# The memory's normalisation and the first cross attention's keys projected at the program's start

## What is computed

```python
# first layer's start: modulation from c, a product with a 1024 x 9216 matrix per layer
mod = silu_c @ w_ada[layer] + b_ada[layer]
h = modulate(rmsnorm(x, norm_g[layer, 0]), sh1, sc1)
x = x + 0.5 * g1 * swiglu(h, ffn_w1[layer, 0], ffn_w3[layer, 0], ffn_w2[layer, 0])
...
# each of the four layers of the second kind, after its mixer
x = x + memory_cross_attention(rmsnorm_2(x, ln_xattn[i]), rmsnorm_2(mem, ln_mem[i]),
                               xa_q[i], xa_kv[i], xa_o[i]).astype(x.dtype)
```

## Time and profile before

| | |
|---|---|
| Time, median of 3 runs | 3674.41 us (3674.11 to 3675.62) |
| The profiled execution, its time | 3674.21 us |
| its span | 3672.5 us |
| PE busy | 3623.0 us, 99% |
| DVE busy | 1836.2 us, 50% |
| ACT busy | 747.8 us, 20% |
| mean granted clock of PE | 0.995 |
| bytes moved | 599 MB, 163 GB/s over the span |

### The profile page before, as it was taken

One profiled execution on the slowest core, in us unless ns is written; L12 is line 12 of the kernel. 1 busy time (PEld: TensorE's weight loads), 2 busy tenths in 40 slices (PEclk: granted clock), 3 DMA queues, 4 the chain that ended last, 5 costly groups with the idle time before them and its releaser, 6 DMA issues.

```text
span 3672.5 us, 46373 instructions
## 1 busy us (share of the span) xinstructions
PE 3623.0 (99%) x20180; PEld 2754.1 (75%) x20180; DVE 1836.2 (50%) x3184; ACT 747.8 (20%) x1468; POOL 15.6 (0%) x43
## 2 busy tenths in 40 slices
PE   7999999999999999999999999999999999999999
PEld 6946696894679587588866679677667977757795
DVE  7854387683536445125732227547412663532384
ACT  1004300101520053211121211033311113421110
POOL 1000000000000000000000000000000000000000
PEclk9999999999999999999999999999999999999999
DMA  9663478654234433334442334433233443333342
GB/s 389 252 261 127 155 280 315 256 184 169 107 128 161 183 115 115 138 138 154 168 160 92 142 135 161 171 127 115 93 135 119 161 181 141 115 129 146 136 169 103
DMA packets 42490, 598.99 MB, mean 163 GB/s; under 512 B 4736, under 2 KB 4752, under 8 KB 6192
## 3 DMA queue, kind: packets, MB, share of 16 engines
q1 hardware_dynamic: 41024, 589.94, 43.2%
q0 software_dynamic: 1264, 6.10, 0.4%
HBM read 594.97 MB, written 1.05 MB: 162 GB/s over the span
## 4 chain that ended last, share of the span: by engine, by line
PE 97%; DVE 1%; DMA 1%; ACT 0%; issue 0%; SPq 0%; DVEq 0%
PE ps L1366 12%; PE ps L2795 12%; PE ps L616 11%; PE ps L499 9%; PE ps L392 8%; PE ps L478 5%; PE ps L2253 4%; PE ps L519 3%; PE ps L2286 3%; PE ps L812 3%; PE ps L2695 3%; PE ps L1761 2%; PE ps L1781 2%; PE ps L3022 2%; PE ps L1756 2%; PE ps L829 2%
## 5 line engine op out<-in xcount | busy, mean ns | idle before, releaser
L616 PE MATMUL ps<-hT,ring 128*128 128x128 f32 (+1 forms) x3136 | 407.9, 292 | 0.0
L616 PEld LDWEIGHTS ps<-hT,ring 128*128 128x128 f32 x3136 | 392.7, 192 | 18.3 <-issue 3.8
L499 PE MATMUL ps<-ring,aT 128*128 128x512 f32 x784 | 341.5, 593 | 0.0
L499 PEld LDWEIGHTS ps<-ring,aT 128*128 128x128 f32 x784 | 148.0, 190 | 178.4 <-issue 178.2
L478 PE MATMUL ps<-ring,aT 128*128 128x512 f32 x448 | 197.4, 598 | 0.0
L228 DVE SCALAR_TENSOR_TENSOR memT<-big,silu_c,memT 128x512 f32<-128x512 f32 x238 | 178.8, 751 | 8.0
L541 ACT ACTIVATE big<-x 128x1024 f32<-128x1024 f32 x34 | 35.9, 1057 | 698.6 <-DVE x L593 389.9
L2253 PE MATMUL ps<-hT,ring 128*128 128x256 f32 x768 | 171.6, 380 | 0.0
L2253 PEld LDWEIGHTS ps<-hT,ring 128*128 128x128 f32 x768 | 144.9, 190 | 25.6 <-issue 7.6
L478 PEld LDWEIGHTS ps<-ring,aT 128*128 128x128 f32 x448 | 84.8, 192 | 100.8 <-issue 100.8
L2795 PE MATMUL ps<-big 128*128 128x128 f32 x1152 | 140.4, 275 | 0.0
(11 more groups left out here) (575 smaller groups left out, 5701.0 us busy)
## 6 DMA issues: line engine op xcount, KB each, us to landing
ring<-weights_in SPq DMA_DIRECT2D x244, 2048.0 KB, 7.8
big<-ada_in SPq DMA_DIRECT2D x34, 2048.0 KB, 8.1
ring<-ada_in SPq DMA_DIRECT2D x2, 2048.0 KB, 26.4
big<-b_gate_in POOLq DMA_DIRECT2D x1, 1536.0 KB, 17.5
x<-x_in SPq DMA_DIRECT2D x1, 1024.0 KB, 4.9
big<-b_gate_in POOLq DMA_DIRECT2D x1, 1024.0 KB, 8.7
big<-mem_in POOLq DMA_DIRECT2D x1, 1024.0 KB, 5.3
out<-big SPq DMA_DIRECT2D x2, 512.0 KB, 2.6
```

The lines of the kernel that those rows point to most:

```text
L499: last = pe.matmul(ps[:, 2 * t + half, :], aT[:, 4 * c + k, t * P:(t + 1) * P], w[:, k, half * 512:(half + 1) * 512], start=first, stop=(4 ...
L616: last = pe.matmul(ps[:, bank + m // 2, (m % 2) * SEQ + at:(m % 2) * SEQ + at + n], w[:, k, m * P:(m + 1) * P], hT[:, k, at:at + n], start ...
```

## The change

The memory is the first load of all and goes to `aT`. ACT and DVE normalise it ahead of x, PE transposes it first, and ACT and DVE take it out of PSUM twice: multiplied by the first cross attention's gain (`early_gained`) and plain (`early_mem`). PE projects the keys of cross attention 0 with two chunks that now lead the list of weights, so that all later chunks have numbers higher by 2 until cross attention 0. The transposes of x stand between the two key chunks; the reductions of slices 0 and 2 stand before the last quarter of the second.

GpSimd's queue writes memory and keys to device memory (`spill`, 2 MB in three parts) and only then issues the small loads, which wait for slice 3 in place of slice 2. memT is read back where the memory was loaded before, and the keys after the last tile of the first mamba is turned. All slices have two places in `big`, so slice 1 waits for the sum of slice 0, and slice 3 for that of slice 2. The ring holds chunks only. In `up_right_dve` of the first swiglu DVE waits for the spill. The fourth swiglu has no work on the memory. `down_pe` 6 ends without keys, and `xattn_pe` 0 projects the queries per token half with `first_channels_pe`.

```diff
+            mem_pe(pe)
+            pe.wait_ge(mem_act_done, 4)
+            pe.wait_ge(mem_dve_done, 4)
+            for j in range(2):
+                w = arrived(pe, j).rearrange("p (k c) -> p k c", k=KT)
+                for m in range(4):
+                    if (j, m) == (1, 3):
+                        pe.wait_ge(down_k_done, 1)
+                        for a in (0, 2):
+                            ada_reduce_pe(pe, a, ada_bank(4 + a // 2))
+                    for k in range(KT):
+                        last = pe.matmul(ps[:, 4 + 2 * j + m // 2, (m % 2) * SEQ:(m % 2 + 1) * SEQ], w[:, k, m * P:(m + 1) * P], early_gained(k), start=(k == 0), stop=(k == KT - 1))
+                last.then_inc(chunks_used, 1)
+                for t in range(TT if j == 0 else 0):
+                    pe.wait_ge(norm_dve_done, 3 * t + 3)
...
-            pool.wait_ge(ada_loaded[2], 16)
+            pool.wait_ge(mem_act_done, 4)
+            pool.wait_ge(mem_dve_done, 4)
+            pool.dma_start(spill[:, 0:2048], early_mem.rearrange("p k c -> p (k c)")).then_inc(mem_moved, 16)
+            for j in range(2):
+                pool.wait_ge(down_k_done, j + 1)
+                pool.dma_start(spill[:, 2048 + 1024 * j:3072 + 1024 * j], early_keys(j).rearrange("p m c -> p (m c)")).then_inc(mem_moved, 16)
+            pool.wait_ge(ada_loaded[1], 32)
...
-            if a >= 4:
-                sp.wait_ge(ada_step, 8 * ada_turn(a - 4) + 8 if a < 6 else 8 * (a - 1))
+            turn = ada_turn(a)
+            if turn >= 2:
+                sp.wait_ge(ada_step, 8 * (turn - 1))
...
             up_ready(dve, i)
+            if i is None:
+                dve.wait_ge(chunks_used, 2)
+                dve.wait_ge(mem_moved, 48)
...
         def keys_pool(pool):
+            pool.wait_ge(mix_turned, 4)
+            pool.dma_start(view(big, 2048, 2048), spill[:, 2048:4096]).then_inc(keys_loaded, 16)
...
         def xattn_pe(pe, n, i, c0):
-            for j in range(2):
+            if n == 0:
+                first_channels_pe(pe, i, c0)
+                pe.wait_ge(keys_loaded, 16)
+            for j in range(2 if n else 0):
...
+            sp.dma_start(view(aTf, 0, TT, D), mem_in.rearrange("(t p) d -> p t d", p=P)).then_inc(mem_loaded, 16)
+            sp.dma_start(col[:, :], col_in).then_inc(columns_loaded, 16)
+            chunk_load(sp, 0)
             sp.dma_start(x[:, :, :], x_in.rearrange("(t p) d -> p t d", p=P)).then_inc(x_loaded, 16)
-            sp.dma_start(col[:, :], col_in).then_inc(columns_loaded, 16)
-            for a in (0, 2):
-                ada_load(sp, a)
-            for c in range(2):
-                chunk_load(sp, c)
-            for a in (1, 3):
-                ada_load(sp, a)
+            ada_load(sp, 0)
+            chunk_load(sp, 1)
+            ada_load(sp, 2)
+            chunk_load(sp, 2)
+            ada_load(sp, 1)
+            chunk_load(sp, 3)
+            ada_load(sp, 3)
```

More of the change, by code:

```diff
@@ L672, in mem_take_act @@
                 for k in range(4 * g + 2, 4 * g + 4):
-                    last = act.copy(memT[:, k, :], ps[:, 2 * g + 1, (k % 2) * SEQ:(k % 2 + 1) * SEQ])
+                    turned = ps[:, 5 + 2 * g, (k % 2) * SEQ:(k % 2 + 1) * SEQ]
+                    act.activation(early_gained(k), turned, ACT.Identity, scale=column('ln_mem_2', k))
+                    last = act.copy(early_mem[:, k, :], turned)
                 last.then_inc(mem_act_done, 1)
@@ L691, in mem_take_dve @@
                 for k in range(4 * g, 4 * g + 2):
-                    last = dve.tensor_copy(memT[:, k, :], ps[:, 2 * g, (k % 2) * SEQ:(k % 2 + 1) * SEQ])
+                    turned = ps[:, 4 + 2 * g, (k % 2) * SEQ:(k % 2 + 1) * SEQ]
+                    dve.tensor_scalar(early_gained(k), turned, column('ln_mem_2', k), None, ALU.mult)
+                    last = dve.tensor_copy(early_mem[:, k, :], turned)
                 last.then_inc(mem_dve_done, 1)
@@ L1417, in first_halves_pe @@
             for j in range(2):
+                if j and not half:
+                    pe.wait_ge(down_k_done, 2)
                 w = (ring[:, (c0 + j) % R, :] if half else arrived(pe, c0 + j)).rearrange("p (k c) -> p k c", k=KT)
@@ L1470, in swiglu_dve @@
             for j in range(11):
-                if mem and j == 2:
-                    mem_take_dve(dve)
                 if j >= 2:
@@ L3278, in _ @@
-            mamba_pe(pe, 0, 5, c0=86)
-            down_pe(pe, 6, None, c0=98, nk=16, kc0=102, ki=0, late=(mamba_turn_pe, 0, 0))
+            swiglu_pe(pe, 0, None, c0=2, ada=range(4, 11))
+            down_pe(pe, 0, (swiglu_dve_done, 10), c0=13, nk=22, ada=range(10, 17), then=(swiglu_dve_done, 11))
+            attn_pe(pe, 0, 0, c0=19)
+            down_halves_pe(pe, 1, 26, [[(attn_act_done, 1), (attn_dve_done, 1)], [(attn_act_done, 2), (attn_dve_done, 2)]], attn_turn_out_pe, (0,))
+            swiglu_pe(pe, 1, 1, c0=28, ada=range(17, 24))
@@ new lines, in _ @@
+            down_pe(pe, 2, (swiglu_dve_done, 21), c0=39, nk=22, ada=range(23, 30), then=(swiglu_dve_done, 22))
+            swiglu_pe(pe, 2, 2, c0=45, ada=range(30, 36))
+            down_pe(pe, 3, (swiglu_dve_done, 32), c0=56, nk=22, then=(swiglu_dve_done, 33), seven=0, taken=(gated_out, up_out_count(2, 10, 5)))
+            attn_pe(pe, 1, 3, c0=62)
+            down_halves_pe(pe, 4, 69, [[(attn_act_done, 3), (attn_dve_done, 3)], [(attn_act_done, 4), (attn_dve_done, 4)]], attn_turn_out_pe, (1,))
@@ L3280, in _ @@
+            swiglu_pe(pe, 3, 4, c0=71)
+            down_pe(pe, 5, (swiglu_dve_done, 43), c0=82, nk=22, then=(swiglu_dve_done, 44), seven=1, taken=(gated_out, up_out_count(3, 10, 5)))
+            mamba_pe(pe, 0, 5, c0=88)
+            down_pe(pe, 6, None, c0=100, nk=16, late=(mamba_turn_pe, 0, 0))
             xattn_pe(pe, 0, 6, c0=104)
@@ L3417, in down @@
             yield _wide(w, j)
+    for j in range(2):
+        yield _tall(g["xa_kv_2"][0], _ranges(512 * j))
     for l in range(2):
```

164 lines of the change are left out of this document (79 added, 85 removed).

## The result

| | before | after |
|---|---|---|
| Time, median | 3674.43 us (3674.11 to 3675.62, 4 runs) | 3653.10 us (3651.85 to 3653.68, 4 runs) |
| The profiled execution, its time | 3674.21 us | 3653.68 us |
| its span | 3672.5 us | 3651.6 us |
| bytes moved | 599 MB, 163 GB/s | 603 MB, 165 GB/s |

The ratio of the two is 0.9937, with a 95% interval of 0.9925 to 0.9949: 21.3 us less. The forecast was 3654, with a range of 3647 to 3665.

What follows compares the result with a forecast made beforehand. PE was taken to bound the kernel, busy 3623.0 of 3672.5 us. Terms 1 and 2 save 34.5 us, term 3 costs 13.9, so 20.6 less than 3674.2 is 3653.6, plus 0.2 for the median: 3654, range 3647 to 3665.

Steps and rivals of the forecast that it cites:

- Term 1: Cross attention 0: keys leave PE's later path, 27.6 us saved, less 1.0 for queries projected per token half.
- The cover: Cross attention 0: 64 narrow query records, 7.2 us, hide token half 1's normalisation with 3.3 us to spare.
- Term 2: Fourth swiglu: memory's transposes 1.75, PE's wait for memT copies 3.22 and low clock 2.9 go; 7.9 us saved.
- Term 3: Start: memory and keys done first on PE make the end of the second halves 13.9 us later, 83.1 against 69.2.
- What was to be hidden: Start: slice 3's sum ends at 61.1, 2.6 us to spare; the spill hidden with 10 us to spare.
- Rival 1: Start, second halves: clock stays up over reductions and wait, 1.8 us less, 3652; chance 0.09.
- reductions and wait again: Start, ahead of the second halves: 3.8 us without dense work lower the clock again, costing 1.8 us.
- Rival 2: Start: clock falls also at x's transposes or reductions inside the keys, 2.9 to 3.4 us each, 3657 to 3660; chance 0.17.
- Rival 4: Cross attention 0 doesn't shrink by the keys because the cover is too short: 6.3 us, 3660; chance 0.05.
- Rival 5: Start: the clock doesn't rise there at all, PE work at half rate, slower at 3710; chance 0.04.
- Rival 3: Start: slice 3 binds instead of PE once its sum ends later than 63.7; 3655 to 3671; chance 0.12.
- spread for shifted falls: Whole kernel: forecast's own spread, 3650 to 3657, includes clock falls shifting elsewhere, 3.4 us each; chance 0.50.

Runs made afterwards that it cites:

- wide_queries: Kernel after, with cross attention 0's queries projected for all tokens at once behind both transposes, so without the cover; 3668.92 us.
- copies_first: Kernel before, with DVE's copies of memT in the fourth swiglu ahead of its sums for chunk 3; 3668.5 us.
- fill_gap: Kernel after, with 18 matmul records of constants in the 2.2 us gap ahead of the second halves, and reductions sharing one PSUM bank; 3651.03 us.
- side_loads_early: Kernel after, with row, rope and gate biases (1.9 MB) issued right behind the memory's spill instead of after slice 3; 3659.82 us.
- gaps_and_warm: keys_in_gaps with warm_start's constants added at the start; 3652.5 us.
- warm_start: Kernel after, with 60 matmul records of constants on PE ahead of the memory's transposes; 3662.46 us.
- keys_in_gaps: Kernel after, with the last two quarters of the keys' second chunk moved into the two gaps at the start, their spill later; 3651.01 us.
- after_again: The changed kernel, unchanged, timed once more beside the reordered one on one chip; 3653.23 us, 6 runs.

## Why the prediction was right

**Term 1** (27.6 less 1.0, 26.6): measured 56.13 - 29.46 = 26.67. The cover held: the normalisation of token half 1 ends at 1557.74 and PE comes to its transposes at 1560.97, 3.2 us later, where 3.3 were reckoned. wide_queries showed what is lost without it.

**Term 2** (7.9): measured 7.98. No wait and no low clock are left at this place (window 1098.20 to 1105.00 after: PE busy throughout, clock 1.00), and copies_first showed that the wait and the fall behind it were one item of 6.2 us.

**Term 3** (13.9 later): measured 13.80, with small errors that cancel. Taking the memory out of PSUM left PE idle for 1.68 us, where 1.6 were put, and with the scaling's end at 11.12 the keys began at 16.59, 0.2 later than reckoned. The low clock over the first keys cost 1.8 us (3.55 for eight records where 1.73 is the full rate, from the next row), not 2.5. The rest up to the end of the reductions took 0.4 more than reckoned: a pair of them and the step back to dense work are nearer 1.8 us than 2 x 0.81. That the sum is so close is luck: the low clock over the first keys comes and goes by 1.8 us between executions (fill_gap and wide_queries didn't have it). The marks behind came within 0.1: end of the reductions at 65.2, second halves at 67.44, first own reduction at 83.02.

**What was to be hidden** was. Slice 3's sum ended at 60.38 for the 61.1 reckoned. Here the prediction misread its own chain: 63.7 is where the pair of reductions begins, and slice 3's is the second of it, 0.8 later, so it had 3.4 us to spare and not 2.6; 3.9 were measured. DVE did not wait for the spill, though its last part was issued at 51.1, as reckoned. A part of 0.5 MB took 7.4 us to land, more than the 5.9 that the prediction took as the upper bound, and the spare time covered it. side_loads_early and gaps_and_warm showed how thin the cover of slice 3 is: 3.9 us decide, from the DMA's side and from PE's.

**The clock.** Rival 1 fell: at 67.90 the clock was at 0.50, and 1.7 us were lost, as forecast. The step "reductions and wait again" is borne out by fill_gap, where 13.9 us replaced 15.6, and limited by warm_start, where the same gap did no harm, so the fall is a likely outcome and no certain one. Rival 2 fell too: behind the transposes of x (33.98) and the reductions inside the keys (46.04) eight records took 1.7 and 1.8 us, the full rate. Rival 4 fell with term 1. Rival 5 fell with the row at 20.14, whose eight records took 1.7 us: the clock had risen. Rival 3 did not occur, and its deciding point was put 0.8 us too early.

**The sum** of the three terms was -20.6, and the marks give -20.85 (26.67 + 7.98 - 13.80). The span shrank by 20.9, since the 1.7 us lost between 1111 and 1546, where the new fall at 1313.80 lies, were nearly won back behind the scores (1.6), where the kernel after has 6.8 us at the low level and before had 13.6. PE worked for 11.7 of those 13.6 us and for all of the 6.8, so half of the difference, 2.4 us by this estimate, more than covers the 1.6; the 0.8 between them stay open. Nothing in the prediction said that the two would cancel, and this is luck too; its spread for shifted falls covered them.

**The two rules weighed.** The Trainium skill's 358 GB/s per core (HBM Reference, Specifications), by which slice 3 would have landed at 63, isn't what this core had: slice 3 was in at 54.4, and a window of the start after shows 435 GB/s at 67.90. The Trainium skill's warning of idle gaps alone (TensorE: Matmul & The Clock Gate, Why this matters for your kernels), by which the 2.2 us would be harmless, fits one of the eight profiled executions with the gap open, warm_start's, and not the seven others; and it doesn't cover the falls without idle time below.

## What to carry over

Work that depends on nothing can be moved into a gap that a load leaves, and its price is then what it pushes back beyond the gap: here 26.7 us moved for 10.3. Look first at what the moved work drags along: the copies that made PE wait could be had for the move of one line, and the small loads had to leave the way of the slices, since slice 3's sum was only 3.9 us ahead of PE. And once an engine is at 99%, differences of 2 or 3 us are to be read from a stage's mark, because later falls of the clock come and go by as much.

## What the runs showed of the hardware that was not expected

**The clock fell with no idle time at all, at matmuls of 32 columns.** The earlier trace rows showed it once. After has it in another stage, the first mamba, timeline:

```profile
1310.37 3.75 PE L2274 MATMUL ps<-small,hT 128*128 128x32 f32 x32
...
3064.23 3.66 PE L2274 MATMUL ps<-small,hT 128*128 128x32 f32 x32
```

The low window from 1313.80 above begins as the first of them end, and the one from 3068.20 behind the second, PE busy throughout. Before ran the same records at 1304.67 without a fall, and after ran those of gdn, where before fell, without one. Which of these places falls differs from kernel to kernel, and between executions of one: keys_in_gaps fell at 2399.20, its repeat didn't. Each of the twelve profiled executions runs three such groups, and at 17 of the 36 the clock fell in the group's last 1.5 us or within 0.6 us behind it, with no wait of PE between. What decides between them the traces don't show.

**A low level can stay for 17 to 20 us of unbroken work when this work is small matmuls.** It is the gdn stage, where three groups of 32 records with operands of 64 x 64 stand in a row. fill_gap's profiled execution, 3663.14 us, timeline and window:

```profile
2597.36 4.47 PE L905 MATMUL ps<-big 64*64 64x128 f32 x29 [1.11 <-ACT big L1051]
...
2608.16 6.39 PE L915 MATMUL ps<-big 64*64 64x128 f32 x29
2614.48 6.43 PE L897 MATMUL ps<-big 128*128 128x128 f32 x32
2620.84 3.38 PE L905 MATMUL ps<-big 64*64 64x128 f32 x29
```

```profile
2599.50:2620.00 20.50, 20.50 (x105) 20.17 (x104) 4.14 (x6) 3.91 (x7) 0.00 (x0) 0.50 0.17 73
```

The 29 records of L915 take 6.39 us here and 3.33 in the kernel after, those of L905 3.38 once the clock has risen, and the 32 of full size 6.43 for 3.84 in the kernel after. PE was busy for the whole of the 20.5 us, so about 10 us are lost. The clock rose again only while the full-sized records ran. wide_queries' profiled execution, 3668.82 us, has the same from 2608.50 for 17.1 us. The other ten profiled executions haven't it, though the wait of 1.11 us ahead of the first group stands in the kernels before and after too. That the longer executions of all kernels are this stretch is likely by its size, but only these two were profiled. The two of the changed kernel at 3670.4, 17 us above the rest, are neither of the outcomes that after_again's expectation named (3662 to 3664, or none). They weren't profiled, but their mean granted clock was 0.993 where the other four had 0.998. 0.005 of 3668 us is some 18 us of work: the lower clock accounts for them by its size, and more than one such stretch is needed; where it lay stays open.
